# Last tile's router turns in free PSUM banks, expert picks in two parts, and two VectorE copies given to ScalarE

## The reference, cut to what matters

```python
x = x + concat([a, c, s]) @ w_out              # output projection, residual
h2 = rms_norm(x, ln2_g)
g_logits = h2 @ gw + gb ; g_idx = argmax(g_logits)      # 4 groups
e_logits = (h2 @ ew + eb)[group g_idx]                  # 8 experts of the group
top_v, top_i = top_k(e_logits, 2)
gate = softmax(g_logits)[g_idx] * softmax(top_v)
expert = g_idx * 8 + top_i
# per expert: y = (silu(xb @ w_gate) * (xb @ w_up)) @ w_down, weighted by gate, added to x
```

## Time and profile before

| | |
|---|---|
| median of 3 runs | 1241.51 us |
| profiled execution | 1242.07 us, span of its trace 1240.2 us |
| TensorE matmul busy | 1141.3 us (92%) |
| VectorE, ScalarE, GpSimd busy | 468.8, 360.1, 289.6 us |
| mean granted TensorE clock | 0.964 |

### The profile page before, as it was taken

One profiled execution on the slowest core, in us unless ns is written; L12 is line 12 of the kernel. 1 busy time (PEld: TensorE's weight loads), 2 busy tenths in 40 slices (PEclk: granted clock), 3 DMA queues, 4 the chain that ended last, 5 costly groups with the idle time before them and its releaser, 6 DMA issues.

```text
span 1240.2 us, 16198 instructions
## 1 busy us (share of the span) xinstructions
PE 1141.3 (92%) x5022; PEld 548.9 (44%) x5023; DVE 468.8 (38%) x1003; ACT 360.1 (29%) x731; POOL 289.6 (23%) x227
## 2 busy tenths in 40 slices
PE   6999999998899999983799999988999999999990
PEld 5897444464356666653333333322333333333330
DVE  3550039932455666317333233222322323323313
ACT  3121100015455555400122332322223223232223
POOL 0110299910000000100221222222122122122123
PEclk9999999999899999995899999989999999999996
DMA  7127111012411111186492799999889999999317
GB/s 252 27 40 136 34 35 35 0 68 73 170 47 56 52 52 52 52 322 238 160 408 72 289 375 375 418 408 411 328 323 382 389 408 377 402 380 393 116 21 274
DMA packets 86157, 261.95 MB, mean 211 GB/s; under 512 B 31927, under 2 KB 49086, under 8 KB 61518
## 3 DMA queue, kind: packets, MB, share of 16 engines
q1 hardware_dynamic: 68868, 243.43, 51.0%
q0 software_dynamic: 11520, 16.81, 6.1%
q10 hardware_dynamic: 5706, 0.92, 0.4%
HBM read 244.86 MB, written 26.74 MB: 219 GB/s over the span
## 4 chain that ended last, share of the span: by engine, by line
PE 87%; DMA 4%; DVE 3%; ACT 2%; issue 1%; DVEq 1%; POOL 0%; SPq 0%; ACTq 0%; POOLq 0%
PE psum L1304 27%; PE psum L1323 13%; PE psum L1029 13%; PE psum L1215 9%; PE psum L1026 4%; PE psum L1173 3%; DMA W<-in_w_gate 3%; PE psum L1292 3%; PE psum L1193 2%; PE psum L1024 2%; PE psum L1311 2%; PE psum L1184 2%; PE psum L1237 1%; DMA W<-in_x 1%; PE psum L1229 1%
## 5 line engine op out<-in xcount | busy, mean ns | idle before, releaser
L1304 PE MATMUL psum<-W,RD 128*64 x800 | 369.2, 605 | 14.2 <-DVE RD L1791 14.2
L1305 PE MATMUL psum<-W,RD 128*64 128x512 f32 x800 | 369.2, 605 | 0.0
L1304 PEld LDWEIGHTS psum<-W,RD 128*64 128x64 f32 x800 | 106.7, 139 | 226.0 <-issue 220.1
L1323 PE MATMUL psum<-W,RD 128*64 x400 | 184.0, 603 | 2.2 <-ACT RD L952 2.2
L1324 PE MATMUL psum<-RD 128*64 128x512 f32 x400 | 184.1, 603 | 0.0
L697 POOL DMA_INDIRECT x_rows<-RD,tabi x49 | 79.4, 1621 | 447.7 <-ACT RD L959 438.0
L1772 DVE TENSOR_TENSOR RD<-psum,RD 128x256 f32<-128x256 f32 x50 | 21.2, 425 | 415.5 <-ACT RD L948 415.5
L1029 PE MATMUL psum<-W 128*128 128x512 f32 x384 | 166.4, 593 | 0.6 <-ACT W L782 0.6
L1215 PE MATMUL psum<-W,RD 128*128 128x512 f32 x256 | 119.3, 600 | 5.3 <-DVE W L1589 4.2
L1029 PEld LDWEIGHTS psum<-W 128*128 128x128 f32 x384 | 72.5, 190 | 89.7 <-issue 88.7
L1305 PEld LDWEIGHTS psum<-W,RD 128*64 128x64 f32 x800 | 106.7, 139 | 0.0
(11 more groups left out here) (319 smaller groups left out, 1263.9 us busy)
## 6 DMA issues: line engine op xcount, KB each, us to landing
W<-in_w_up SPq DMA_DIRECT2D x32, 2048.0 KB, 13.2
W<-in_w_gate SPq DMA_DIRECT2D x32, 2048.0 KB, 18.3
W<-in_w_down SPq DMA_DIRECT2D x32, 2048.0 KB, 20.3
W<-in_x SPq DMA_DIRECT2D x16, 512.0 KB, 4.7
W<-in_w_in SPq DMA_DIRECT2D x5, 1024.0 KB, 11.6
W<-in_w_in SPq DMA_DIRECT2D x16, 256.0 KB, 4.3
x_rows<-W SPq DMA_DIRECT2D x8, 512.0 KB, 2.9
h_rows<-RD SPq DMA_DIRECT2D x8, 512.0 KB, 3.5
```

The source lines that it names most:

```text
L1304: pe.matmul(bank(2)[0:HALF].rearrange("p (g n) -> p g n", g=2), x, near, start=k == 0, stop=k == KD - 1)
L1305: ins = pe.matmul(bank(2)[HALF:P], x, upgate1[:, k].rearrange("p g n -> p (g n)"), start=k == 0, stop=k == KD - 1)
L1323: pe.matmul(out[0:HALF], a, W[:, bass.ds(base + (2 * KD * FF + D * k), 512)], start=k == 0, stop=k == FK - 1)
```

## The change

1. Halves j = 13 and 15 of the output projection go to bank 3, half 14 stays in bank 7; j = 13 waits for the last softmax (e_ok), 14 and 15 for the addition before the previous one.
2. Tile 7's turns go to banks 0 and 1, its logits to bank 2, its h2T to a buffer of its own (xr). Turn (7,0) moves to step k = 39, between the two halves of the last fill; the logits of tile 7 start after the first half of h2T. VectorE writes the logits of tile 6 one step later.
3. Tile 7's h2 is scaled by ScalarE, no longer by VectorE.
4. The picks are a function `picks(lo, hi, done)`, called for tiles 0 to 5 at k = 36 and for tiles 6 and 7 after the loop's last logits. MM, mbf, esel and the small routing vectors move from RD to RG. The waits for x2_out and h2_out come after the picks.
5. ScalarE copies the second 64 columns of the slot one-hot from the first (sl_ok, sl_two); L1720 goes.
6. For block 0 ScalarE copies the up and gate weights, after tab_ok, and no engine reads the table of block 0.

```diff
+LAST_FILL = 8 + 4 * NT - 1
+def lg_bank(i):
+    return 5 if i < NT - 1 else 2
+def proj_bank(j):
+    return 3 if j in (13, 15) else 7
...
+        h2Tl = xr[:, :].rearrange("p (k n) -> p k n", k=KD)
...
# ScalarE, after the loop
+            act.wait_ge(ms2_ok, NT)
+            act.wait_ge(rstd2_ok, NT)
+            act.activation(mixT[:, :, (NT - 1) * P:L], x2[:, (NT - 1) % 3, :].rearrange("p (c n) -> p c n", c=KD),
+                           ACT.Copy, scale=rstd2[:, NT - 1:NT]).then_inc(h2_ok, 1)
             act.wait_ge(gd_ok, 1)
             act.activation(rrv("gexp"), rrv("gdif"), ACT.Exp)
             act.activation(rrv("eexp"), rrv("edif"), ACT.Exp).then_inc(ge_ok, 1)
+            for r in range(2):
+                c = slice(8 * r, 8 * r + 8)
+                act.wait_ge(sl_ok, r + 1)
+                act.activation(slot1h[:, c, HALF:P], slot1h[:, c, 0:HALF], ACT.Copy).then_inc(sl_two, 1)
+            act.wait_ge(wug_in[0], 32)
+            for r in range(2):
+                act.wait_ge(tab_ok, r + 1)
...
+                act.activation(first_dst, first_src, ACT.Copy).then_inc(ex_cu, 1)
...
# TensorE, fill
-                    if part == 0 and not own and 2 * i + half:
-                        pe.wait_ge(x2_ok, 2 * i + half)
+                    j = 2 * i + half
+                    if part == 0 and not own:
+                        if j == 13:
+                            pe.wait_ge(e_ok, 2 * NI)
+                        elif j:
+                            pe.wait_ge(x2_ok, j if j < 13 else j - 1)
...
# TensorE, x2_turn
+                if i == NT - 1:
+                    pe.wait_ge(x2_ok, 2 * i + b + 1)
+                    pe.wait_ge(e_ok, 2 * NI)
...
# TensorE, logits
-                pe.wait_ge(h2T_ok, i + 1)
...
+                    if c == 0:
+                        pe.wait_ge(h2T_ok if i < NT - 1 else h2T_half, i + 1)
+                    if c == 4:
+                        pe.wait_ge(h2T_ok, i + 1)
...
# TensorE, loop
                 fill(k, 0)
...
+                if k == LAST_FILL:
+                    x2_turn(NT - 1, 0)
                 fill(k, 1)
...
# TensorE, table
                     pe.wait_ge(tab_ok, r // 8 + 1)
+                    pe.wait_ge(sl_two, r // 8 + 1)
...
# VectorE, loop
+                if i is not None and i < NT - 2:
+                    logit_evac(i)
+                if k == LAST_FILL - 3:
+                    dve.wait_ge(x2_ok, 2 * NT - 2)
+                    dve.wait_ge(x2_out[2], 32)
+                    dve.wait_ge(const_ok, 4)
+                    for r in range(2):
+                        dve.tensor_scalar(tokv[:, 8 * r:8 * r + 8], tokf[:, :], 2.0, 2.0 * L * r - 4.0 * L, ALU.mult, ALU.add)
+                    link(dve.memset(g8, -3e38))
+                    picks(0, NT - 2, False)
+                if k == LAST_FILL:
+                    x2_turned(NT - 1, 0)
+                if k == LAST_FILL + 1:
+                    logit_evac(NT - 2)
+                    x2_turned(NT - 1, 1)
+                    x2_var(NT - 1)
+                    dve.wait_ge(rstd2_ok, NT)
+                    logit_evac(NT - 1)
+                    picks(NT - 2, NT, True)
...
# VectorE, tables
-                dve.tensor_tensor(slot1h[:, c, HALF:P], bc(slot[:, c].unsqueeze(2), [P, 8, HALF]), bc(iotaf[:, 0:HALF].unsqueeze(1), [P, 8, HALF]), ALU.is_equal)
+                   .then_inc(sl_ok, 1)
...
# VectorE, expert step
-                base, loads = tables(b)
                 if not first:
+                    base, loads = tables(b)
                     act_mul(b)
...
+                if not first:
+                    dve.tensor_copy(dst[:, :, 4:8], src[:, :, 4:8]).then_inc(ex_cu, 1)
```

More of the change, by code:

```diff
@@ L938, in down_copy @@
             def down_copy(base, loads, used):
-                for n in range(SLOTS):
-                    act.wait_ge(wd_in[n], loads[n])
+                for n, need in enumerate(loads):
+                    act.wait_ge(wd_in[n], need)
                 if used is not None:
@@ L1236, in logits @@
                 for c in range(KD):
-                    ins = pe.matmul(bank(5)[:, 0:36], h2T[:, c, :], rw[:, c, :], start=c == 0, stop=c == KD - 1)
+                    if c == 0:
+                        pe.wait_ge(h2T_ok if i < NT - 1 else h2T_half, i + 1)
+                    if c == 4:
+                        pe.wait_ge(h2T_ok, i + 1)
+                    ins = pe.matmul(bank(lg_bank(i))[:, 0:36], (h2T if i < NT - 1 else h2Tl)[:, c, :], rw[:, c, :], start=c == 0, stop=c == KD - 1)
                 ins.then_inc(lg_ps, 1)
@@ L1258, in _ @@
                     i = tile_at(k, 13 + b)
-                    if i is not None:
+                    if i is not None and (i < NT - 1 or b):
                         x2_turn(i, b)
@@ L1588, in x2_half @@
                         dve.wait_ge(x2_out[i % 3], 16 * (i // 3))
-                dve.tensor_tensor(x2[:, i % 3, cols], bank(7), xa[:, i % 2, cols], ALU.add).then_inc(x2_ok, 1)
+                dve.tensor_tensor(x2[:, i % 3, cols], bank(proj_bank(2 * i + half)), xa[:, i % 2, cols], ALU.add).then_inc(x2_ok, 1)
             def x2_turned(i, b):
                 dve.wait_ge(h2T_ps, 2 * i + b + 1)
-                if i and b == 0:
+                if i and b == 0 and i < NT - 1:
                     dve.wait_ge(lg_ok, i)
-                dve.tensor_tensor(h2T[:, 4 * b:4 * b + 4, :], bank(5).rearrange("p (k n) -> p k n", k=4),
+                to, src = (h2T, bank(5)) if i < NT - 1 else (h2Tl, bank(b))
@@ L1603, in _ @@
                 i = tile_at(k, 13)
[L1604 to L1606 removed]
+                if i is not None and i < NT - 1:
+                    x2_var(i)
                 if k < NI:
@@ L1651, in _ @@
             gate = rrv("gate").rearrange("p (r t) -> p r t", r=2)
-            idx = rrv("idx").rearrange("p (r t) -> p r t", r=2)
-            row, stp, slot, tokv = (rrv(x, 16) for x in ("row", "stp", "slot", "tokv"))
-            link(dve.memset(g8, -3e38))
-            link(dve.tensor_copy(g8[:, :, 0:4], logit[:, :, 0:4]))
-            for i in range(NT):
-                ins = dve.max(mx8[:, i, :], g8[:, i, :])
-            link(ins)
-            for i in range(NT):
-                ins = dve.max_index(gi8[:, i, :], mx8[:, i, :], g8[:, i, :])
@@ L1684, in _ @@
-            dve.tensor_tensor(mbf, MM[:, 0:8, :], MM[:, 8:16, :], ALU.add).then_inc(mm_ok, 1)
+            row, stp, slot = (rrv(x, 16) for x in ("row", "stp", "slot"))
+            dve.tensor_tensor(gdif, logit[:, :, 0:4], bc(mx8[:, :, 0:1], [P, NT, 4]), ALU.subtract)
+            dve.tensor_tensor(edif.unsqueeze(2), me8[:, :, 1:2], me8[:, :, 0:1], ALU.subtract).then_inc(gd_ok, 1)
+            for s in range(3):
+                dve.wait_ge(x2_out[s], 16 * ((NT - 1 - s) // 3 + 1))
+            dve.wait_ge(h2_out, 16 * NT)
```

117 lines of the change are left out of this document (77 added, 40 removed).

## The result

The changed kernel takes 1231.61 us, the median of four runs (1231.27 to 1234.07), beside 1242.01 us for the kernel before in the same comparison. The ratio is 0.9915, 95% interval 0.9902 to 0.9928: 10.4 us faster, where 16.9 were forecast. The direction was right, the time lies 0.6 us above the stated range. The profiled execution of after took 1231.33 us, its span is 1229.6 us.

A forecast was written before the change was run, and what follows sets the result against it. TensorE bounds the kernel up to 557 us, then one serial routing chain to 599.5 us. Terms 4.5 + 7.1 + 4.6 - 0.5 + 0.6 + 0.55 = 16.85 us gave 1224.6 us; range 1221.3 to 1229.4, widened to 1220.5 to 1231.

The forecast's parts named there:

- part 1: Output projection: halves 13, 14 and 15 no longer wait for the half just before; 4.5 us gained, bounds 3.7 and 4.5.
- part 2: Last tile's turns and logits: one-by-one handovers and stops go, logits of tile 7 at full clock; 7.1 us gained.
- part 3: Picks of tiles 0 to 5 made ahead in VectorE's idle time; 4.6 us gained, bounds 3.8 and 5.3.
- part 5: One-hot's second half copied by ScalarE, off VectorE's way to the first table matmul; 0.6 us gained, bounds 0 and 0.6.
- Part 4: Behind the picks, row write and gates delay taking the ranks; 0.5 us lost, bounds 0.2 and 2.
- Step 6: Block 0 without table reads, weights copied by ScalarE: starts 0.55 us earlier, bounds 0 and 0.6; nothing waits for ScalarE there.
- the upper side of the gain: Table matmuls and block 0's first six pairs at full clock would give 2 to 3 us more: 1221.3 us.
- rival D: First expert blocks: clock stays low past block 0's sixth pair, 0.42 us per pair; two blocks 1244.9 us; chance 0.02.
- the poor end of all terms: Every term of the sum at its low bound: gain 12.1 us, giving 1229.4 us.
- Rival B: Picks of tiles 0 to 5 hold up tile 6's chain by their full 6.3 us: 1231.0 us; chance 0.06.
- rival A: Tile 7's row write lands late, at 570.45 us, delaying the ranks: gain 7.2 us, 1234.3 us; chance 0.08.

The follow-up runs named there:

- e12: Changed kernel with ScalarE's reads of block 0's table entries kept and block 0's weights copied by VectorE at constant addresses; 1227.17 us.
- e1: Changed kernel plus one tiny one-column Silu on ScalarE right behind the exponentials; 1228.19 us.
- e8: Changed kernel with e1's Silu, e6's waits, and transposes of a constant into unused bank 3 at four places in TensorE's idle stretches; 1222.55 us.
- e6: Changed kernel with VectorE's four waits for the row writes (x2_out, h2_out) moved behind the exponentials and gates; 1229.74 us.
- e3: Kernel before with only one part of the change: ScalarE uses constants for block 0 and doesn't read the table; 1246.04 us.
- e7: Changed kernel, late table load kept, with 28 transposes of a constant tile into an unused bank between blocks 0 and 1; 1229.42 us.
- e2: Changed kernel with ScalarE alone reading block 0's table entries again, as before the change; 1225.95 us.
- e11: Changed kernel with the edits of e2 and e6 together; 1229.13 us.

## Why the prediction was wrong

**Steps 1 to 5** held. With the 1.33 us of late start taken off, each against its forecast: part 1 brings logits 6 to 551.67 us (551.6); part 2 empties logits 7 at 555.99 (555.8); part 3 takes 4.0 us (4.0), its first call 6.5 (6.3) with 2.5 us in hand (2.6); part 5 takes 0.60 off the way from L1694's place to the table (0.6). Part 4 was small by half: L1773 starts at 562.26 and not at 561.7, mostly because the write took 4.4 us and not 3.9. That is 0.5 us.

**Step 6** is the one that failed, in the sentence that VectorE's and ScalarE's reads of block 0's table are just removed. For VectorE that was right, even more than I took: from the first transposes to the first pair 1.66 us against 2.55, 0.9 and not 0.55, 0.36 of it because the transposes ran at the high clock (0.77 us for 1.13), which is luck. For ScalarE I weighed only the two copies, asked whether something waits for them, and left out what else stands on ScalarE there: a table load of 1.28 us whose cover was the time between its place and the wait for block 0. The reads had kept the two waits apart. The load wasn't in my rows at all, although ScalarE's timeline of before shows it at 596.64 us. Moved behind block 0, it costs 1.36 us of longer stop and 2.5 us of low clock in block 1 (the other 0.3 of the 4.2 us is one more slow pair in block 0). Without these 3.9 us the changed kernel would have stood at about 1227.7 us, inside the range.

**The clock** was the second error, and a larger one in microseconds. I took the low clock of block 0's pairs into the upper side of the gain only, and named the drop as rival D with a price from 40 pairs on. What happened is rival D in small: about six more pairs at 0.85 us in block 1, 2.5 us by the stretch. The point from which it decides was a stop of TensorE, and I had costed nothing for making one longer.

**The range** had 12.1 us as the poor end of all terms. It was built from the terms of the sum, and the lost 4.2 us are of a term that was not in it. Rival B, which gives 1231.0 and so nearly the measured time, is refuted, since nothing waited for the first picks: a time that fits isn't a mechanism. Two slips changed no mechanism: rival A says that VectorE reaches its wait for h2_out 15 us sooner, where its own times give 8 (567.7 and 559.8 us), and 1224.6 less the 3 us of the good side is 1221.6, not 1221.3.

**What stays open.** The 1.33 us before 520 us: 0.39 by 322 us and 0.94 between 322 and 360, where the clock rises from 0.50 at 338.41 us before and 340.44 us after. In the fourteen traces the second tile's fill roughly follows that rise (358.86 us for the earliest, 337.82, and 361.44 for the latest, 341.58). Two of them start with the program of before, and both are the earliest (358.91 and 358.86); the twelve others lie between 359.12 (e12) and 361.44 (e1), a spread of 2.3 us with the same code up to there. So most of the 1.33 us can be chance; whether the changed program adds a shift of its own isn't shown.

## What to carry to other kernels

When an instruction that costs nothing is removed, look at what stood in its cover and at what it kept apart: the order of the engine's instructions, with their waits, shows it before any run. A table load has a place of its own, and a one-column activation right behind the last use of the old table pins it there, for 0.20 us of a ScalarE that was idle (e1). And where TensorE's work comes in short pieces with stops between, cost a longer stop twice, once for itself and once for the matmuls behind it at half rate; transposes into an unused bank in such stretches bought 5.6 us here, by the medians of e8 and e1 from two comparisons, of which about 0.7 us is e6's edit.

## What the runs showed of the hardware

- A table load put in for an activation can stand behind one of the waits ahead of it (changed kernel, e3, e7). Load and Silu then take 1.28 + 0.38 us behind the event, not 0.38.
- TensorE's granted clock fell to 0.50 in or shortly behind every idle stop of 3.6 to 3.7 us before block 1 (seven traces), with two of five of 2.2 to 2.4 us, and with neither of the two filled with transposes (e7, e8). It did not always fall at once: in e3 the first three pairs behind the stop were still fast.
- The rise is as irregular as the fall: block 0 has five to seven slow pairs before the clock is up again in thirteen traces, and none in e8, whose transposes ran ahead of it.
- A single profile is not a mean: the time from block 0 to the first down matmul was the same program's 24.91 and 25.07 us, but 20.9 and 22.6 us for e2 and e11, which differ only in the place of four waits ahead of the ranks; the difference is slow pairs. Medians move too: 1231.61 and 1230.28 us for the same program.
